# Prompt mixer: element-wise work of VectorE given to ScalarE

## The reference, cut to what matters

```
xn = rmsnorm(x, norm_mix)
(a_gate, a_x, b_q, b_k, b_v, b_qi, b_ki, b_wi, c_q, c_k, c_v, c_g, c_a) = split_cols(xn @ w_in)
# group a (RG-LRU)
u = conv_b;  for j in range(4): u = u + xc[:, j:j + T] * conv_w[j]
r, i = sigmoid(u @ rg_wa + rg_ba), sigmoid(u @ rg_wx + rg_bx)
log_a = -8 * r * softplus(-rg_lambda);  a = exp(log_a)
b = sqrt(-expm1(2 * log_a)) * i * u
h = linear_scan(a, b, h0);  y_a = gelu(a_gate) * h
# group b (sparse attention): 8 query heads, 4 key heads of 64
q, k = partial_rope(rmsnorm(b_q, q_norm), pos), partial_rope(rmsnorm(b_k, k_norm), pos)
score = index_scores(qi, ki, wi);  attention over the 256 best keys of each query
# group c (gated linear attention), chunk by chunk, with a state S
x = x + concat(y_a, y_b, y_c) @ w_out
x = x + relu(rmsnorm(x, norm_mlp) @ w_up)^2 @ w_down
```

## Time and profile before

| | |
|---|---|
| median of three runs | 4403.04 us (4398.36 to 4406.07) |
| profiled execution | 4405.4 us, span 4403.7 us |
| mean granted TensorE clock | 0.865 |
| busy: PE, PEld, DVE, ACT, POOL | 83%, 62%, 49%, 23%, 11% |
| prompt mixer of layer 0 | from the start to about 997 us |
| prompt mixer of layer 1 | from about 2205 to 3197 us |

### The profile page before, as it was taken

The page is one execution under the profiler, slowest core; times in us unless marked ns, Lnnn a source line. Parts: engine busy times, 40 slices in busy tenths (PEclk is TensorE's granted clock), DMA queues, the critical chain, the costliest instruction groups (busy, mean ns, idle before and its releaser), DMA issues.

```text
span 4403.7 us, 52598 instructions
## 1 busy us (share of the span) xinstructions
PE 3642.5 (83%) x17978; PEld 2744.9 (62%) x17978; DVE 2137.6 (49%) x4901; ACT 1028.7 (23%) x2273; POOL 476.6 (11%) x639
## 2 busy tenths in 40 slices
PE   5878878787558999999958787886875689999999
PEld 3545555464324999999835455554543349999997
DVE  1357778835513433443413577788355134434434
ACT  2233333214301121112022333332152011211110
POOL 0100000022200000000001000000222000100000
PEclk9888887558789999999978888786587799999999
DMA  3000000173431111111130000001744311111111
GB/s 127 18 15 13 13 11 8 31 78 116 130 119 59 36 51 39 39 58 39 50 121 16 17 13 13 11 8 33 76 122 130 111 61 39 48 39 39 58 39 51
DMA packets 180191, 230.68 MB, mean 52 GB/s; under 512 B 80946, under 2 KB 146548, under 8 KB 177876
## 3 DMA queue, kind: packets, MB, share of 16 engines
q1 hardware_dynamic: 158324, 170.23, 14.1%
q0 software_dynamic: 21600, 57.08, 4.1%
HBM read 203.74 MB, written 23.50 MB: 52 GB/s over the span
## 4 chain that ended last, share of the span: by engine, by line
PE 68%; DVE 16%; issue 5%; ACT 4%; DVEq 3%; DMA 1%; POOLq 1%; SPq 1%; POOL 1%; ACTq 0%; another core or an unknown queue 0%
PE bank L1325 12%; PE bank L1326 12%; PE bank L1327 12%; PE bank L1035 10%; DVE arena L1386 6%; PE bank L1317 6%; PE bank L1031 5%; PE bank L1133 3%; PE bank L1117 2%; ACT arena L665 1%; DVE arena L1652 1%; SPq L425 1%; PE bank L1221 1%; PE bank L1125 1%; PE bank L1079 1%
## 5 line engine op out<-in xcount | busy, mean ns | idle before, releaser
L1794 DVE TENSOR_TENSOR x_and_hraw<-x_and_hraw,bank 128x512 f32<-128x512 f32 (+1 forms) x576 | 396.1, 688 | 631.2 <-PE bank L1327 631.2
L665 ACT ACTIVATE arena<-bank 128x512 f32<-128x512 f32 (+11 forms) x926 | 348.0, 429 | 865.3 <-PE bank L1035 325.0
L1035 PE MATMUL bank<-arena 128*128 128x512 f32 (+5 forms) x1440 | 525.1, 520 | 3.2 <-ACT arena L692 1.7
L1386 DVE TENSOR_SCALAR_CACHE_REDUCE arena<-arena,vectors 128x384 bf16<-128x384 f32 (+6 forms) x434 | 500.2, 1152 | 34.4 <-issue 2.5
L1325 PE MATMUL bank<-xT_hi,w_up_hi 128*128 128x364 f32 (+1 forms) x1536 | 506.9, 330 | 3.2 <-DVE vectors L1775 3.2
L1326 PE MATMUL bank<-xT_lo,w_up_hi 128*128 128x364 f32 (+1 forms) x1536 | 506.6, 330 | 0.0
L1327 PE MATMUL bank<-xT_hi,w_up_lo 128*128 128x364 f32 (+1 forms) x1536 | 506.6, 330 | 0.0
L1325 PE MATMUL bank<-w_down_hi,hidden_hi 128*128 128x512 f32 x1152 | 450.4, 391 | 7.5 <-issue 7.5
L1326 PE MATMUL bank<-w_down_lo,hidden_hi 128*128 128x512 f32 x1152 | 449.9, 391 | 0.0
L1327 PE MATMUL bank<-w_down_hi,hidden_lo 128*128 128x512 f32 x1152 | 449.6, 390 | 0.0
L1035 PEld LDWEIGHTS bank<-arena 128*128 128x128 f32 (+1 forms) x1440 | 253.7, 193 | 254.4 <-issue 225.0
(11 more groups left out here) (248 smaller groups left out, 4399.4 us busy)
## 6 DMA issues: line engine op xcount, KB each, us to landing
w_up_landing<-in_w_up SPq DMA_DIRECT2D x32, 1024.0 KB, 7.4
w_down_landing<-in_w_down SPq DMA_DIRECT2D x32, 1024.0 KB, 4.9
arena<-in_w_in SPq DMA_DIRECT2D x16, 1322.0 KB, 17.7
arena<-in_cache_k SPq DMA_DIRECT2D x128, 128.0 KB, 2.9
arena<-in_cache_v SPq DMA_DIRECT2D x128, 128.0 KB, 2.9
arena<-in_cache_k POOLq DMA_DIRECT2D x128, 128.0 KB, 2.9
arena<-in_cache_v POOLq DMA_DIRECT2D x128, 128.0 KB, 2.9
arena<-in_cache_ki SPq DMA_DIRECT2D x256, 32.0 KB
```

Of the source, the lines that this page charges most:

```text
L665: return act.activation(dst, src, ACT.Copy, scale=scale)
L1035: ins = mm(b[:R, o:o + w], xnT[:, c, 0:R], w_in[:, c, c0:c0 + w], start=c == 0, stop=c == 7)
L1386: ts(junk, sc, cf[:R].bitcast(F32), None, ALU.is_ge, ALU.add, accum_out=cnt[:R])
L1794: tt(x, x, b[P - R:P, :], ALU.add).then_inc(s_took, 1)
```

## The change

Five pieces of work go from VectorE to ScalarE. The scaling of x by its inverse root (`norm_x`) becomes a Copy with a scale from memory, at h=1 behind the exponential of head 1, for tile 0 directly behind its square. The squares of the heads become a Square on ScalarE, placed behind G3 of the same tile (for tile 0: behind all eight parts of its projection), with a new semaphore `s_sqr`; VectorE keeps the reduction. The first tap of the convolution becomes an Identity with scale and bias, directly behind the evacuation of C0, together with the square of the gate (its factor 0.044715 is taken in by the scale). a*a becomes a Square at the end of `gates`, after a drain, and the signal for VectorE comes after it. In the gelu VectorE keeps one operation of three.

```diff
@@ block.scalar
+                def norm_x(t):
+                    R = rows(t)
+                    act.wait_ge(s_rstd, TT3(l, 0, t) + 1)
+                    act.activation(xb[:R, :], xb[:R, :], ACT.Copy, scale=small[:R, 16:17]).then_inc(s_xn, 1)
+
+                def head_squares(t):
+                    R = rows(t)
+                    if t:
+                        act.wait_ge(s_ossq, T(l, t))
+                    act.activation(sq[:R], hb[:R, 0:12, :], ACT.Square).then_inc(s_sqr, 1)
+
+                def first_tap(t):
+                    R = rows(t)
+                    if t == NT:
+                        act.wait_ge(s_st, 16 * 19 * (l + 1))
+                    act.drain()
+                    for h in range(2):
+                        src = ax[:, h, 0:P] if t < NT else axs[:, h, :, 0:ST]
+                        uo = u[:, h, 0:R] if t < NT else u[:, h, 0:R].rearrange("p (b t) -> p b t", b=SB)
+                        act.activation(uo, src, ACT.Identity, bias=vecs[:, h:h + 1], scale=convw[:, 0, h:h + 1])
+                    act.activation(gl[:, :, 0:R], ag[:, :, 0:R], ACT.Square, scale=0.044715 ** 0.5)
...
                             ins.then_inc(s_evac, 1)
+                        first_tap(t)
...
-                        ins = act.activation(b2[:, h, 0:R], th[:, h, 0:R], ACT.Tanh, bias=vecs[:, 11 + h:12 + h], scale=vecs[:, 11 + h:12 + h])
-                    ins.then_inc(s_thr, 1)
+                        act.activation(b2[:, h, 0:R], th[:, h, 0:R], ACT.Tanh, bias=vecs[:, 11 + h:12 + h], scale=vecs[:, 11 + h:12 + h])
+                    if t == NT:
+                        act.wait_ge(s_yst, T(l, NT))
+                    act.drain()
+                    act.activation(hh[:, :, 0:R], la[:, :, 0:R], ACT.Square).then_inc(s_thr, 1)
...
                 square(0)
+                norm_x(0)
                 for i in range(8):
                     project(0, i)
+                head_squares(0)
...
                         if h == 0 and N_:
                             square(s + 1)
+                        if h == 1 and N_:
+                            norm_x(s + 1)
...
                         if h == 8:
                             if N_:
                                 project(s + 1, 7)
+                                head_squares(s + 1)
@@ block.vector
-                def head_squares(t):
-                    R = rows(t)
-                    v.wait_ge(s_evac, A_AT[l, t, "G2"] + 1)
-                    tt(sq[:R], hb[:R, 0:12, :], hb[:R, 0:12, :], ALU.mult)
-                    D_()
+                def head_sums(t):
+                    R = rows(t)
+                    v.wait_ge(s_sqr, T(l, t) + 1)
                     v.tensor_reduce(small[:R, 32:44], sq[:R], AXX, ALU.add).then_inc(s_kssq, 1)
...
-                        ts(uo, xs(0), convw[:, 0, h:h + 1], vecs[:, h:h + 1], ALU.mult, ALU.add)
-                        D_()
...
-                    tt(gl[:, :, 0:R], ag[:, :, 0:R], ag[:, :, 0:R], ALU.mult)
-                    D_()
-                    ts(gl[:, :, 0:R], gl[:, :, 0:R], 0.044715, 1.0, ALU.mult, ALU.add)
-                    D_()
-                    tt(gl[:, :, 0:R], gl[:, :, 0:R], ag[:, :, 0:R], ALU.mult).then_inc(s_gin, 1)
+                    stt(gl[:, :, 0:R], gl[:, :, 0:R], 1.0, ag[:, :, 0:R], ALU.add, ALU.mult).then_inc(s_gin, 1)
...
-                    for h in range(2):
-                        tt(hh[:, h, 0:R], la[:, h, 0:R], la[:, h, 0:R], ALU.mult)
-                    D_()
```

More of the change, by code:

```diff
@@ L375, in program @@
         s_ssq, s_rstd, s_xn = sem("square_sum"), sem("rstd"), sem("xn_ready")
-        s_kssq, s_krs, s_hb = sem("head_squares"), sem("head_rstd"), sem("heads_ready")
+        s_sqr, s_kssq, s_krs, s_hb = sem("heads_squared"), sem("head_squares"), sem("head_rstd"), sem("heads_ready")
         s_u, s_gin, s_b2, s_bc = sem("conv_ready"), sem("gelu_inner"), sem("one_minus_a2"), sem("gate_sums")
@@ L1429, in _ @@
                 D_()
-                def norm_x(t):
+                def head_sums(t):
                     R = rows(t)
-                    v.wait_ge(s_rstd, TT3(l, 0, t) + 1)
-                    v.wait_ge(s_x, 16 * (l * TILES + t + 1))
-                    ts(xb[:R, :], xb[:R, :], small[:R, 16:17], None, ALU.mult).then_inc(s_xn, 1)
-                def head_squares(t):
-                    R = rows(t)
-                    v.wait_ge(s_evac, A_AT[l, t, "G2"] + 1)
-                    tt(sq[:R], hb[:R, 0:12, :], hb[:R, 0:12, :], ALU.mult)
-                    D_()
+                    v.wait_ge(s_sqr, T(l, t) + 1)
                     v.tensor_reduce(small[:R, 32:44], sq[:R], AXX, ALU.add).then_inc(s_kssq, 1)
@@ L1489, in gelu_inner @@
                     R = rows(t)
-                    tt(gl[:, :, 0:R], ag[:, :, 0:R], ag[:, :, 0:R], ALU.mult)
-                    D_()
-                    ts(gl[:, :, 0:R], gl[:, :, 0:R], 0.044715, 1.0, ALU.mult, ALU.add)
-                    D_()
-                    tt(gl[:, :, 0:R], gl[:, :, 0:R], ag[:, :, 0:R], ALU.mult).then_inc(s_gin, 1)
+                    stt(gl[:, :, 0:R], gl[:, :, 0:R], 1.0, ag[:, :, 0:R], ALU.add, ALU.mult).then_inc(s_gin, 1)
                 def one_minus_a2(t):
                     R = rows(t)
-                    if t == NT:
-                        v.wait_ge(s_yst, T(l, NT))
                     v.wait_ge(s_thr, T(l, t) + 1)
-                    for h in range(2):
-                        tt(hh[:, h, 0:R], la[:, h, 0:R], la[:, h, 0:R], ALU.mult)
-                    D_()
                     stt(b2[:, :, 0:R], hh[:, :, 0:R], 1.0, b2[:, :, 0:R], ALU.add, ALU.mult)
@@ L1658, in head_max @@
                     ts(small[:, 64 + h % 2:65 + h % 2], small[:, 70:71], -0.125, None, ALU.mult).then_inc(s_nb, 1)
-                norm_x(0)
                 for s in range(NST):
@@ L1671, in _ @@
                         if h == 0 and P_:
[L1672 to L1677, removed]
+                            head_sums(s)
+                        if h == 1 and P_:
+                            conv(s)
                         if h == 2 and P_:
```

## The result

The changed kernel took 4432.4 us (median of five runs, 4422.9 to 4434.3) against 4399.8 us for the kernel before in the same comparison: ratio 1.0069, 95% interval 1.0053 to 1.0085, so slower by 23 to 37 us. That is inside the range on record (4403 to 4436), slower as forecast, and about 10 us above the predicted time; it lies nearer to the 4434 us of rival 3 than to the 4422.5 us of the sum. As a difference the sum was +19.5 us, which lies just outside the measured 23 to 37.

A forecast was written before the change was run, and what follows sets the result against it. Neither VectorE nor TensorE was taken as full, since they hand work to each other, so waits were followed head by head. Terms of +45.5 and -26.0 gave +19.5 us on the 4403.04 median: 4422.5, range 4403 to 4436.

The forecast's parts named there:

- rival 3: Delays cost more: longer TensorE idle stretches run more of G0 at 1.2 GHz, 1 us in each of 12 steps; 4434; chance 0.13.
- the sum: The prediction's own case, all terms added: +45.5 and -26.0 make +19.5 us, forecast 4422.5; chance 0.68.
- Step 0: Tile 0's squares wait behind all eight projections, so its heads end late with TensorE idle: +10.0 us a layer, +20.0.
- Tile 0's scaling: Tile 0's normalisation takes 1.13 us on ScalarE against 0.75 on VectorE: +0.35 a layer, +0.7.
- Head 0: Squares delay GpSimd's root in steps 1 to 3, +5.1; VectorE's run shortens in steps 4 to 7, -8.2, and step 8, -1.4.
- Head 1: VectorE sheds two taps and the normalisation before head 2's maximum: -12.2 in steps 3 to 6, -2.2 in 7, +0.4 in 2.
- Behind C0: Drain, two taps and a Square, 1.25 us, ahead of the copy TensorE waits for, steps 2 to 7: +13.3.
- Gates: Drain and square of a between the gates and the copy TensorE waits for: +0.5 in steps 2 to 7, +6.0.
- steps 4 to 7: each 0.5 to 1.3 us shorter: A sign expected in the profile after: each of these prompt-mixer steps shortens by that much.
- The bounds: Unknowns around the sum: taps -4 to +3, step 0 -2 to +3, savings passed on 0 to +5; 4414 to 4433.
- Rival 1: VectorE paces steps 3 to 8, so all it sheds comes through, 4.0 us x 12: -20.0, 4383.0; chance 0.07.
- Rival 2: ScalarE's additions in gates and taps are hidden and cost nothing: +0.2, 4403.2; chance 0.12.

The follow-up runs named there:

- e2: The kernel before with only the squares of the heads moved to ScalarE, placed as in the change: ratio 1.0027.
- e3: The kernel before with only the scaling of x moved to ScalarE, as in the change: ratio 0.9986.
- e5: The kernel before with only the square of a moved to ScalarE, at the end of the gates: ratio 0.9997.
- e9: e6 with the square of a back on VectorE: ratio 0.9959 against the kernel before.
- e1: The changed kernel with tile 0's head squares behind G2 instead of behind G3: ratio 1.0046 against the kernel before.
- e4: The kernel before with only the first tap and the gate's square on ScalarE, behind C0, and the shorter gelu: ratio 1.0018.
- e12: e7 with the taps and the gate's square also on ScalarE, behind head 4's probabilities: ratio 0.9976 against the kernel before.
- e8: e1 with the drain, taps and gate's square done twice: ratio 1.0100 against the kernel before.
- e7: e3 with tile 0's scaling back on VectorE and tile 1's behind step 0's copies of the transposed heads: ratio 0.9952 against the kernel before.
- e6: e1 with the taps and the gate's square moved behind the copies of head 4's probabilities: ratio 0.9985 against the kernel before.

## Why the prediction was right, and what its sum missed

**Step 0, +20.0 forecast:** +9.9 and +10.0 us in the two layers' traces, times at each point within 0.1 us, and e2 pins it to the squares. The size was that of the earlier trace rows.

**Tile 0's scaling, +0.7:** too small to be told in the whole. The step missed *tile 1's* scaling in step 0, 2.2 us a layer (e3: 1.01 of standing and 1.15 of scaling), hidden in the change behind step 0's own delay.

**Head 0.** Steps 1 to 3: TensorE's wait before the heads' transposes grew by 0.74 to 1.15 us each, 4.9 in six steps (5.1 forecast). Steps 4 to 7: down by 0.4 to 1.4 each, 7.5 in eight (8.2 forecast). Step 8: -3.4 (-1.4 forecast).

**Head 1, -14.0 in all:** 32.7-18.3 = 14.4 us less idle before the probabilities' transposes; e3, which has the scaling alone, shows 12.4 of it. That the totals agree is partly luck. The forecast had 1.1 to 1.5 us in each of ten steps; measured are 0.2 to 1.8 in eight of them and 4.0 and 4.3 in steps 3 and 5 of layer 1, and in these two e5, which has no part of this term, shows 2.8 and 4.1 less as well. Only about 6 us are there without them.

**Behind C0, +13.3:** the wait grew by 1.17 to 1.27 us in steps 2 to 6 and by 0.32 in step 7 (0.5 forecast): 13.0 us in twelve steps.

**Gates, +6.0:** in the changed kernel the wait grew by 3.8 us in twelve steps, 2.6 of it in the two steps 7 (1.09 to 3.20 in layer 0) and 1.3 in step 6 of layer 1. Alone it is 10.0 (e5), worth no time; in company its removal gave 11 us (e9).

**What failed** is the sum's assumption that a wait costs its own length (outside step 0): "Steps 3 to 7 pass on between all and four fifths of what VectorE saves", with the clock left to rival 3 at 1 us a step. The sum had no term for TensorE's busy time but the cold start of step 0, in the 22.0 us taken from step 1. Of the +25.6 us that the profiles show, 4.5 are that start. 10.7 lie in steps 2 to 7, and step 7 of layer 1, where the kernel before was faster than every other, alone has 10.2; so the kernel before is a poor measure here. Against the mean of the ten kernels without taps behind C0 (938.3 us, 932 to 943) steps 2 to 7 have 9.1 us more. The rest is in step 1 (1.7), in steps 8 to 10 (3.7) and outside the mixers' steps (5.0), where TensorE's idle time fell by more. Outside step 0 the mixers' steps lost 4.2 us in the profiles where the sum had -1.2, and the medians put the whole 10 us above it. Rival 3 named the mechanism and put its price at +12; for steps 2 to 7 that size fits (9 us in the change, 15 in e1, 16 in e4, by the same mean), and the sum and the rival are both true in part.

The sign "steps 4 to 7: each 0.5 to 1.3 us shorter" did not come: from one set of head transposes to the next these steps changed by between -4.9 and +6.7 us, mostly with TensorE's busy time; their waits at head 0 fell as forecast. The bounds also left out a part of the sum: with step 8's own 2 us either way they come to 4414.5 to 4435.5, not 4414 to 4433.

The four parts alone add up to 1.0027, 0.9986, 1.0018 and 0.9997: +0.28%. Together they made +0.69%. The 0.41%, 18 us, belongs to no part. In the profiles the gap lies in steps 8 to 10: the squares, the scaling, the taps and the square of a alone shorten these by 14.1, 11.5, 18.0 and 4.2 us, and all of them together by 3.6. This is also why the same taps alone (e4) left TensorE's total busy time as it was: in steps 2 to 7 they raised it as in e1. What makes the matmuls of steps 8 to 10 take 285 us in one kernel and 311 in another stays open, and with one profile of each kernel so does whether it belongs to the kernel or to the execution.

**Rival 1** is out: it needs 3 us and more from every one of steps 4 to 7, and of these eight two won that much (-3.4 in step 5 of layer 0, -4.9 in step 6 of layer 1), both with less busy time; and e9 and e12, with ScalarE's additions in easier places and without the cost of step 0, come to 0.996 to 0.998 and not lower. The Trainium skill's advice on it ("Perfetto Trace Analysis", Optimizing Scalar/DVE Operations: ScalarE as a relief for a saturated VectorE) did not come into play, as VectorE is 77% busy in step 7. The Trainium skill's preference for VectorE in multiplications ("ScalarE: Activation LUTs", Rules for kernel authors) the trace bears out for durations only (1.15 us for the scaling against 0.75); for the time of the kernel the place decided: e7, with that slower multiplication on ScalarE, is as fast as any kernel here. **Rival 2** is out for the taps: the waits of e4 and e8 grew by what was added, and the time with them. For the square of a alone it holds in time (e5), though not in the wait.

## What to carry to other kernels

Where TensorE waits for ScalarE, work handed to ScalarE goes behind the copy that TensorE wants; moving the same activations from in front of such a copy to a place in the queue where they made TensorE wait no longer gave 27 us, of which the profiles put some 22 in the steps concerned. Work that was done as its data arrived should not be queued behind the rest of its stage: the first tile has no cover. And add up TensorE's busy time for the same matmuls beside its idle time, stage by stage. A total can hide an effect (e4) or show one that lies in stages which the change doesn't touch (e6, e12), and one profiled execution is one sample: compare it with the median and the clocks of the others.

## What the runs showed of the hardware

The same 32 matmuls of G2 took 6.21 us at 1.00 and 7.90 us at 0.79, behind a wait 1.3 us longer and a C0 that had itself fallen from 1.00 to 0.84. Waits of 1.2 to 1.3 us more, put into steps 2 to 6 ahead of G2, came with 9 to 16 us more of TensorE's busy time in steps 2 to 7 of both layers (table: 947.4 to 954.5 against a mean of 938.3), and waits of 2.5 us more (e8) with 31. Over the fourteen kernels of the table idle ranged from 734 to 772 us and busy from 3636 to 3670 for the same work, and less idle did not go with less busy time: e12 is lowest but one in idle and has 19 us more busy than e7. Steps 8 to 10 ran at a granted clock of 0.51 to 0.57 in every kernel, and took 285 to 311 us of busy time for the same matmuls. Which pattern of waits sets the clock there was not found.
